# One 512-column product for both parts of x in the feed-forward stages

## What is computed

```python
def _swiglu(x, w1, w2):
    gt, up = jnp.split(x @ w1, 2, axis=-1)
    return (jax.nn.silu(gt) * up) @ w2        # w1: 1024 x 5632, w2: 2816 x 1024
```

## Time and profile before

| | us |
|---|---|
| median of three executions | 3036.09 |
| the profiled execution | 3034.12 |
| its span | 3032.1 |
| TensorE busy in the span | 2707.2 |
| VectorE busy | 1279.1 |
| ScalarE busy | 995.9 |
| GpSimd busy | 113.6 |

### The profile page before, as it was taken

How to read it: one execution, slowest core, us unless ns; L and a number is a source line. 1 busy time by engine, 2 the same in 40 slices (tenths; PEclk the granted TensorE clock), 3 DMA queues, 4 the chain that set the end, 5 groups by cost and what they waited for, 6 DMA issues and landing times. The chain is left out here.

```text
span 3032.1 us, 40074 instructions
## 1 busy us (share of the span) xinstructions
PE 2707.2 (89%) x16430; PEld 1977.5 (65%) x16430; DVE 1279.1 (42%) x2375; ACT 995.9 (33%) x1640; POOL 113.6 (4%) x44
## 2 busy tenths in 40 slices
PE   8989999999998999999888679999889864989896
PEld 8979886898997988798776334333369542433333
DVE  5555643656556553556765321111144652111112
ACT  4444651444444562344465111111134231111111
POOL 0001000101001000100100100000010010000000
PEclk9999999999999999999898889999999987999999
DMA  9646434464654733554422479999983016999997
GB/s 305 204 118 192 148 91 166 153 208 139 199 182 111 236 98 123 169 195 127 155 98 70 179 281 421 421 421 421 421 313 104 1 42 265 420 421 421 421 421 292
DMA packets 314273, 695.36 MB, mean 229 GB/s; under 512 B 57392, under 2 KB 242608, under 8 KB 264944
## 3 DMA queue, kind: packets, MB, share of 16 engines
q1 hardware_dynamic: 311184, 682.29, 61.4%
q10 hardware_dynamic: 2912, 10.52, 1.1%
HBM read 691.68 MB, written 1.08 MB: 228 GB/s over the span
## 5 line engine op out<-in xcount | busy, mean ns | idle before, releaser
L277 PE MATMUL ps<-xT_upper,weight_parts 128*128 128x256 f32 (+1 forms) x4656 | 865.8, 288 | 29.6 <-DVE xT_lower L896 12.9
L222 DVE TENSOR_TENSOR weight_parts<-ring,weight_parts 128x1024 fp32r<-128x1024 f32 x447 | 578.0, 1297 | 470.6 <-ACT weight_parts L214 470.5
L277 PEld LDWEIGHTS ps<-xT_upper,weight_parts 128*128 128x128 f32 (+1 forms) x4656 | 736.8, 193 | 47.0 <-issue 19.0
L277 PE MATMUL ps<-xT_lower,weight_parts 128*128 128x256 f32 (+1 forms) x2328 | 665.2, 286 | 0.0
L214 ACT ACTIVATE weight_parts<-ring 128x1024 fp32r<-128x1024 f32 x447 | 469.7, 1053 | 570.7 <-PE ps L277 334.2
L277 PEld LDWEIGHTS ps<-xT_lower,weight_parts 128*128 128x128 f32 (+1 forms) x2328 | 449.6, 193 | 0.5
L2596 PE MATMUL ps<-ring,bias_tiles 128*64 128x512 f32 x1024 | 240.4, 596 | 34.6 <-DMA ring<-in_moe_w_gate 18.8
L2596 PE MATMUL ps<-ring,arena 128*64 128x512 f32 x1024 | 239.9, 596 | 33.1 <-DMA ring<-in_moe_w_gate 17.1
L2869 DVE TENSOR_TENSOR bias_tiles<-ps,bias_tiles 128x512 f32<-128x512 f32 x32 | 22.1, 692 | 504.1 <-ACT bias_tiles L2743 504.1
L2646 PE MATMUL ps<-moe_slots,bias_tiles 128*64 128x512 f32 x1024 | 229.0, 595 | 4.4 <-ACT bias_tiles L2746 4.4
L754 PE MATMUL ps<-weight_parts,hidden_upper 128*128 128x512 f32 x704 | 218.2, 391 | 1.7 <-DVE hidden_lower L806 1.7
(11 more groups left out here) (337 smaller groups left out, 2890.5 us busy)
## 6 DMA issues: line engine op xcount, KB each, us to landing
ring<-in_ffn_w SPq DMA_DIRECT2D x132, 1024.0 KB, 5.1
ring<-in_moe_w_up SPq DMA_DIRECT2D x128, 1024.0 KB, 24.3
ring<-in_moe_w_gate SPq DMA_DIRECT2D x128, 1024.0 KB, 24.5
moe_slots<-in_moe_w_down SPq DMA_DIRECT2D x128, 1024.0 KB, 20.3
ring<-in_w_gate SPq DMA_DIRECT2D x24, 1024.0 KB, 7.4
ring<-in_w_in SPq DMA_DIRECT2D x20, 1024.0 KB, 6.7
ring<-in_ssd_w_in SPq DMA_DIRECT2D x20, 1024.0 KB, 5.3
ring<-in_attn_w_qkv SPq DMA_DIRECT2D x18, 1024.0 KB, 9.5
```

Of the source, the lines that this page charges most:

```text
L222: dve.tensor_tensor(self.part(n, 1), cut(self.stream.slot(pos)), self.part(n, 0).bitcast(F32), ALU.subtract).then_inc(self.split, 1)
L277: m = pe.matmul(out[0:rows, :], w[of_w][:, k, :], c.xTp[of_x][:, k, :], start=(k == 0 and (of_w, of_x) == PARTS[0]), stop=(k == KT - 1 and ...
```

## The change

A new function, `wide_products`, takes the place of `feature_products` in the feed-forward stages only. The two parts of x now lie side by side in one tile, so for each k-slice the upper weight part meets both in one product of 512 columns, which fills a bank: columns 0 to 255 get upper by upper, columns 256 to 511 the cross product. The lower weight part meets the upper part of x in a product of 256 columns, as before. Gate and up take a bank each, and a hidden half takes one of two pairs of banks in turn. ScalarE copies the cross product out of the bank (`cross`), VectorE adds it to the other half of the bank into a tile in SBUF (`sums`), for each gate and each up unit. The silu and both multiplications read `sums` in place of PSUM. The wait of TensorE ahead of a hidden half is for `h_full` of the half two before, where it was four before.

```diff
+def wide_products(c, pe, n, bank, fresh=False):
+    w = c.units.both(n)
+    pe.wait_ge(c.units.split, n + 1)
+    for k in range(KT):
+        if fresh and k % 4 == 0:
+            pe.wait_ge(c.x_parts.sem, c.x_parts.at(k // 4 - 1))
+        if k:
+            pe.matmul(bank[:, 0:S], w[1][:, k, :], c.xTp[0][:, k, :], start=False, stop=False)
+        m = pe.matmul(bank, w[0][:, k, :], c.xT_both[:, :, k, :], start=(k == 0), stop=(k == KT - 1))
+        if k == 0:
+            pe.matmul(bank[:, 0:S], w[1][:, k, :], c.xTp[0][:, k, :], start=False, stop=False)
+    m.then_inc(c.units.done, 1)
...
-        self.xTp = [sb(f"xT_{part}", [P, KT, S], F32R) for part in ("upper", "lower")]
+        self.xT_both = sb("xT_parts", [P, 2, KT, S], F32R)
+        self.xTp = [self.xT_both[:, which, :, :] for which in range(2)]
...
+        def side_bank(m, side):
+            return ps[:, 4 + 2 * (m % 2) + side, :]
...
-                if m >= 4:
-                    pe.wait_ge(c.h_full.sem, c.h_full.at(m - 3))
+                if m >= 2:
+                    pe.wait_ge(c.h_full.sem, c.h_full.at(m - 1))
...
+                    if u < 4:
+                        m = 2 * n + u // 2
+                        act.wait_ge(c.units.done, U[6 * n + u] + 1)
+                        if m >= 2:
+                            act.wait_ge(c.h_full.sem, c.h_full.at(m - 1))
+                        act.activation(cross[m % 2][u % 2][:, :], side_bank(m, u % 2)[:, S:2 * S], ACT.Copy).then_inc(c.cross.sem, c.cross.one())
...
-                        act.wait_ge(c.units.done, U[6 * n + u] + 1)
+                        act.wait_ge(c.gate_sum.sem, c.gate_sum.at(m + 1))
...
-                        act.activation(sg[m % 2][:, :], ps[:, 4 + m % 4, 0:S], ACT.Silu).then_inc(c.sg_full.sem, c.sg_full.one())
+                        act.activation(sg[m % 2][:, :], sums[m % 2][0][:, :], ACT.Silu).then_inc(c.sg_full.sem, c.sg_full.one())
...
+                    m, j = 2 * n + u // 2, u // 2
+                    if u < 4:
+                        both = side_bank(m, u % 2)
+                        dve.wait_ge(c.cross.sem, c.cross.at(4 * n + u + 1))
+                        ins = dve.tensor_tensor(sums[m % 2][u % 2][:, :], both[:, 0:S], cross[m % 2][u % 2][:, :], ALU.add)
+                        if u % 2 == 0:
+                            ins.then_inc(c.gate_sum.sem, c.gate_sum.one())
+                        else:
+                            c.dve_chain.link(dve, ins)
...
-                        up = ps[:, 4 + m % 4, S:2 * S]
+                        up = sums[m % 2][1][:, :]
```

More of the change, by code:

```diff
@@ L456, in __init__ @@
         self.x_split = self.counted("x_parts_ready")
+        self.cross = self.counted("cross_products_kept")
+        self.gate_sum = self.counted("gate_sums_ready")
         self.h_hi = self.counted("hidden_upper_part_ready")
@@ L723, in ffn_stage @@
         hid = [sb(f"hidden_{b}", [P, S], F32) for b in range(2)]
+        cross = [[sb(f"{side}_cross_{b}", [P, S], F32) for side in ("gate", "up")] for b in range(2)]
+        sums = [[sb(f"{side}_sum_{b}", [P, S], F32) for side in ("gate", "up")] for b in range(2)]
+        def side_bank(m, side):
+            return ps[:, 4 + 2 * (m % 2) + side, :]
         sg = [sb(f"silu_{b}", [P, S], F32) for b in range(2)]
@@ L740, in hidden @@
                 m = 2 * n + half
-                if m >= 4:
-                    pe.wait_ge(c.h_full.sem, c.h_full.at(m - 3))
+                if m >= 2:
+                    pe.wait_ge(c.h_full.sem, c.h_full.at(m - 1))
                 for side in range(2):
-                    feature_products(c, pe, U[6 * n + 2 * half + side], ps[:, 4 + m % 4, side * S:(side + 1) * S], fresh=(m == 0 and side == 0))
+                    wide_products(c, pe, U[6 * n + 2 * half + side], side_bank(m, side), fresh=(m == 0 and side == 0))
             def down(n, half, t):
@@ L776, in _ @@
                 for u in range(6):
-                    if u in (1, 3):
+                    if u < 4:
                         m = 2 * n + u // 2
@@ L783, in _ @@
                             act.wait_ge(c.h_full.sem, c.h_full.at(m - 1))
-                        act.activation(sg[m % 2][:, :], ps[:, 4 + m % 4, 0:S], ACT.Silu).then_inc(c.sg_full.sem, c.sg_full.one())
+                        act.activation(cross[m % 2][u % 2][:, :], side_bank(m, u % 2)[:, S:2 * S], ACT.Copy).then_inc(c.cross.sem, c.cross.one())
+                    if u in (1, 3):
+                        m = 2 * n + u // 2
[3 more added lines that the diff above has]
+                        act.activation(sg[m % 2][:, :], sums[m % 2][0][:, :], ACT.Silu).then_inc(c.sg_full.sem, c.sg_full.one())
                     if 6 * n + u < 6 * CHUNKS - 2:
@@ L796, in _ @@
                 for u in range(6):
+                    m, j = 2 * n + u // 2, u // 2
[7 more added lines that the diff above has]
+                            c.dve_chain.link(dve, ins)
                     if u in (1, 3):
-                        m, j = 2 * n + u // 2, u // 2
-                        up = ps[:, 4 + m % 4, S:2 * S]
+                        up = sums[m % 2][1][:, :]
                         dve.wait_ge(c.sg_full.sem, c.sg_full.at(m + 1))
```

## The result

The changed kernel takes 3050.97 us in the median (3046.62 to 3053.30), against 3037.41 for the kernel before in the same comparison: a ratio of 1.0045, interval 1.0032 to 1.0058, so 10 to 18 us slower. The profiled execution spans 3048.8 us.

What follows compares the result with a forecast made beforehand. TensorE was taken as the bound, busy 2707 of 3032 us and gapless in steady chunks. -12.4 + 1.8 + 16.2 + 4.8 = +10.4 us gave a median of 3046.5 us (0.34% above 3036.1), range 3030 to 3056.

Steps and rivals of the forecast that it cites:

- The saving: Feed-forward k-slices on TensorE: one product fewer saves 9.0 ns each, 12.4 us in all, bounds 0 and 16.5.
- The steady chunks: Added copies and additions lengthen the chain to `h_full` by 0.46 us, hidden under the first down unit with 0.3 to spare.
- The stage ends: Last chunk of each of four stages: the 0.46 us longer chain shows once, +1.8 us in all.
- The collision: Start of stages two to four: multiplications with two SBUF operands take turns with GpSimd's operations, 3 x 5.4 = +16.2 us.
- the walk: Step-by-step timing of the second stage's start from U1's end: TensorE waits 6.15 us for `h_full`, 0.7 for U6's weights.
- The old waits: Near the start of stages two to four, three TensorE waits for VectorE's lower parts, 1.45 us a stage, disappear.
- The clock: After TensorE's 6 us gap in stages two to four, a spell at 1.2 GHz costs 1.6 us each, +4.8 us.
- The sum: Whole kernel: all forecast terms together, +10.4 us, giving a median of 3046.5 us, 0.34% above 3036.1.
- No new turns: Rival: the multiplications don't meet GpSimd and the three small waits stay; -9.6 us, 3026.5 us, chance 0.13.
- VectorE keeps its turn: Rival: three short operations run together after GpSimd's first, only lower parts alternate; -4.2 us, 3032 us, chance 0.12.
- The clock holds: Rival: all as forecast but no lower clock after the gap; +5.6 us, 3041.7 us, chance 0.15.
- Columns set the pace: Rival: fewer products save nothing, or the page's 3.5 us; 3055 to 3059 us, chance 0.10.

Runs made afterwards that it cites:

- two narrow products: The changed kernel with each 512-column product cut into two of 256 columns into the two halves of the same bank: 3061.5 us, ratio 1.0080.

## Why the prediction was right

**The saving.** Forecast -12.4 us. The term was mis-sized a little, by two errors that partly cancel. A slice saves 355.9 - 348.8 = 7.1 ns and not 9.0, 9.8 us in all: the down units' 228.3 ns, the nearest row, was too cheap a price for a wide product at a unit's border. Against that, two down units take 0.034 us less (medians of the traces), which the sum didn't have: 44 x 0.034 = 1.5 us. Together that is 11.3 us, and a chunk is 16.60 us long, where 16.6 was forecast; that it fits so well is partly luck. The experiment with two narrow products gives 10.5 by the medians. The range of 0 to 16.5 us held it. The Trainium skill ("TensorE: Matmul & The Clock Gate", Back-to-back issue gap), which the prediction weighed, gives its 2.5 ns for a product by itself and says that in a stream of weight loads and products both set the pace. By the Trainium skill's 2.5 ns the saving would have been an estimated 3.5 us: the measurement decides against it.

**The steady chunks.** Forecast: hidden, with 0.3 us to spare. No steady down unit waits. The chain can be measured where it shows, at the stage's end: 2.44 us, as forecast.

**The stage ends.** Forecast +0.46 us each. The chain grew from 1.98 to 2.44 us, the wait from 0.43 to 0.92. No run took this away by itself; it is read from the traces.

**The collision.** Forecast, from the end of U1 (T): GpSimd starts at T + 6.15, `h_full` lets TensorE go at T + 14.3. In the trace U1 ends at about 543.43, where the copy of its cross product begins at 543.46, followed by the table load:

```profile
543.46 0.38 ACT L808 ACTIVATE up_cross<-ps 128x256 f32<-128x256 f32 x1 [1.45 <-PE ps L293]
543.86 1.28 ACT L816 ACT_TABLE_LOAD   x1
545.15 0.42 ACT L816 ACTIVATE silu<-gate_sum 128x256 f32<-128x256 f32 x1
```

The two points are T + 6.2 and T + 14.0. The load stands behind the copy, as the walk had it. From U4's start to U5's it is 8.57 us in place of 2.72, so the gap costs 5.85 us, where the walk had 6.15. Forecast for collision and clock before the old waits are taken off: 3 x (6.85 + 1.6) = 25.4 us; taking GpSimd's work away gives 24.1 by the traces and 25.1 by the medians. One detail of the reading behind it was loose: GpSimd's third operation in rows 6 takes 3.26 us, and 2.35 plus a weight subtraction of 1.22 would be 3.57.

**The old waits.** Forecast 3 x 1.45 = 4.4 us; taking the work away from the kernel before gives 4.7 by the traces and 5.1 by the medians.

**The clock.** Forecast 4.8 us, measured 4.5 by the traces and 4.3 by the medians. The stretches at the lower clock, 3.6 to 5.9 us, lie within the 3.4 to 6.8 that was assumed, but the working was rougher than its result: the 3.4 stands in none of the rows that it names, and the upper bound of 3.0 us a stage leaves out the 0.7 us that it says it takes off.

**The sum.** By the traces -11.3 + 1.8 + 24.1 - 4.7 = +9.9 us, where +10.4 was forecast. In the two profiled executions the four stages together are 11.2 us longer; the remaining 1.3 lies ahead of the first down units, where the changed kernel happened to have 14.7 us at the lower clock and the kernel before 12.1. The medians say +13.6, with an interval of 10 to 18, and the profiled executions differ by 16.7. What is above 11.2 lies outside the feed-forward stages, where the forecast had nothing: there the profiled executions take 2276.2 and 2281.8 us. Most of it is between the first and the second stage, 329.5 and 335.2 us, with a mean granted clock of 0.96 and 0.94. In all traces the time outside is 2276 to 2279 us for the three kernels that start from before, and 2276 to 2283 for the nine others. Whether the change does something to the clock there or this is chance, no run tells.

**The rivals.** *No new turns* and *VectorE keeps its turn* fall with the 2.4 us multiplications: three in a row each waited for another GpSimd operation. *The clock holds* falls with the 0.50 in the stretch behind the gap. *Columns set the pace* falls with the experiment of two narrow products.

## What to carry to other kernels

When an operand moves from PSUM to SBUF, look at who else works at that moment: here the move cost nothing on VectorE alone and 2 us an operation beside GpSimd. Look for the short job off the critical path (GpSimd was busy for 4% of the span before), and price a chain through it in whole instructions of the other engine; small instructions and an operand left in PSUM keep it short. And an idle gap on TensorE has a second price behind it in the granted clock.

## What the runs showed of the hardware that was not expected

Eight fp32r products of 512 columns took 233.8 ns each in feature units and 227 in down units, with narrow ones at 117.5 to 118.6. Neither the layout of the moving columns nor their alternation with narrow products explains it.

What a product costs also depends on what went before it. In the kernel before, down units follow 96 narrow products. The ninth down product stands in its timeline beside rows 2:

```profile
97.95 0.39 PE L754 MATMUL ps<-weight_parts,hidden_lower 128*128 128x512 f32 x1
```

From 96.10 to there eight products take 231 ns each, and the sixteen up to 101.58 take 227. In the changed kernel, where the last products ahead are wide and narrow in turn, all 24 take 227. Why is open.
